# A hybrid decoder layer on one core: low halves and gated sums in turns, a key split and pooling products moved

## The reference, cut to what matters

```python
z = h @ lp['w_in']                       # one combined projection, h = x*(1+s1)+b1
att = forget_attention(q, k_all, v_all, ...)          # 8 heads x 64, prompt causal
conv_out = gb * dwconv3(gc * z_h)                     # 512 channels
pooled = trailing means over 2/4/8/16 tokens - token  # 4 groups of 128 channels
pool_out = einsum(pooled, lp['pool_w']) * lp['pool_scale']
gates = sigmoid(z[..., OFF_G:])                       # 3 gates of 1024 channels
merged = gates0*(att @ w_br_attn) + gates1*(conv_out @ w_br_conv) + gates2*(pool_out @ w_br_pool)
out = merged @ lp['w_o']
x = layer_norm(ALPHA * x + g1 * out)
x = layer_norm(ALPHA * x + g2 * SwiGLU(x*(1+s2)+b2))
```

## Time and profile before

| | us |
|---|---|
| median of 3 runs | 2202.35 (2200.02 to 2204.29) |
| profiled execution, its own time | 2206.09 |
| its span, first to last instruction | 2204.5 |
| PE busy (share of span) | 2047.4 (93%) |
| DVE, POOL, ACT busy | 797.4, 631.7, 389.2 |
| mean granted clock of PE | 0.966 |

### The profile page before, as it was taken

The page is one execution under the profiler, slowest core; times in us unless marked ns, Lnnn a source line. Parts: engine busy times, 40 slices in busy tenths (PEclk is TensorE's granted clock), DMA queues, the critical chain, the costliest instruction groups (busy, mean ns, idle before and its releaser), DMA issues.

```text
span 2204.5 us, 33007 instructions
## 1 busy us (share of the span) xinstructions
PE 2047.4 (93%) x13046; PEld 1941.9 (88%) x13046; DVE 797.4 (36%) x1423; ACT 389.2 (18%) x700; POOL 631.7 (29%) x482
## 2 busy tenths in 40 slices
PE   4989898778899999999999899999999999999996
PEld 3978887544599999999999798999999999999996
DVE  2445445543200042201702547333243323341326
ACT  1434444412110000000110124200000000000003
POOL 5031111042222232323332625323223232232323
PEclk9999998879999999999999899999999999999998
DMA  9232112167523112222111221011111111111112
GB/s 293 95 92 59 30 40 79 42 222 239 178 81 120 39 46 80 79 75 86 46 39 48 67 101 30 29 48 47 39 48 38 48 47 39 48 38 48 48 29 82
DMA packets 175721, 164.18 MB, mean 74 GB/s; under 512 B 15134, under 2 KB 139506, under 8 KB 175499
## 3 DMA queue, kind: packets, MB, share of 16 engines
q1 hardware_dynamic: 153307, 132.50, 19.7%
q0 software_dynamic: 6144, 17.01, 2.4%
q10 hardware_dynamic: 16184, 13.46, 2.0%
HBM read 149.03 MB, written 14.03 MB: 74 GB/s over the span
## 4 chain that ended last, share of the span: by engine, by line
PE 83%; DVE 6%; DMA 3%; SPq 3%; ACT 2%; issue 2%; POOL 1%; ACTq 0%; POOLq 0%; DVEq 0%
PE psA L1699 10%; PE psA L1705 10%; PE psA L1703 10%; PE psB L1705 10%; PE psB L1703 10%; PE psB L1699 10%; DMA kpage<-in_cache_k 2%; PE psB L1965 2%; PE psB L1808 2%; PE ps L1876 1%; PE psA L1862 1%; PE psB L1811 1%; PE psB L1812 1%; DVE prob L1241 1%; PE ps L1931 1%
## 5 line engine op out<-in xcount | busy, mean ns | idle before, releaser
L618 POOL CAST whi<-raw 128x1024 fp32r<-128x1024 f32 x131 | 136.0, 1038 | 1194.1 <-PE psA L1699 568.2
L619 POOL TENSOR_TENSOR wlo<-raw,whi 128x1024 fp32r<-128x1024 f32 x131 | 318.6, 2432 | 10.5
L1699 PE MATMUL psA<-hhi,whi 128*128 128x364 f32 x984 | 218.5, 330 | 4.2 <-DVE alo L1464 2.7
L1705 PE MATMUL psA<-hhi,wlo 128*128 128x364 f32 x984 | 218.8, 331 | 0.0
L1703 PE MATMUL psA<-hlo,whi 128*128 128x364 f32 x984 | 218.3, 330 | 0.0
L1705 PE MATMUL psB<-hhi,wlo 128*128 128x364 f32 x984 | 217.3, 329 | 0.0
L1703 PE MATMUL psB<-hlo,whi 128*128 128x364 f32 x984 | 217.3, 329 | 0.0
L1699 PE MATMUL psB<-hhi,whi 128*128 128x364 f32 x984 | 216.5, 328 | 0.0
L1699 PEld LDWEIGHTS psA<-hhi,whi 128*128 128x128 f32 x984 | 171.1, 189 | 5.0 <-issue 4.7
L1584 DVE TENSOR_TENSOR ft<-psB,sil 128x1092 f32<-128x1092 f32 x22 | 28.5, 1295 | 406.3 <-PE psB L1705 399.4
L1705 PEld LDWEIGHTS psA<-hhi,wlo 128*128 128x128 f32 x984 | 172.3, 189 | 0.0
(11 more groups left out here) (417 smaller groups left out, 3682.2 us busy)
## 6 DMA issues: line engine op xcount, KB each, us to landing
raw<-in_w_in SPq DMA_DIRECT2D x53, 512.0 KB, 3.9
raw<-in_w_gate_up SPq DMA_DIRECT2D x44, 512.0 KB, 3.8
kpage<-in_cache_k SPq DMA_DIRECT2D x64, 256.0 KB, 4.2
vpage<-in_cache_v POOLq DMA_DIRECT2D x64, 256.0 KB, 4.1
ada_late<-in_ada_w SPq DMA_DIRECT2D x8, 2048.0 KB, 8.0
raw<-in_w_down SPq DMA_DIRECT2D x22, 512.0 KB, 3.7
ada<-in_ada_w SPq DMA_DIRECT2D x4, 2048.0 KB, 17.5
x_keep<-xt SPq DMA_DIRECT2D x1, 4368.0 KB, 13.8
```

The source lines that it names most:

```text
L618: link(nc.gpsimd.tensor_copy(whi[slot][:, 0:n, :], raw[slot][:, 0:n, :]))
L619: nc.gpsimd.tensor_tensor(wlo[slot][:, 0:n, :], raw[slot][:, 0:n, :], whi[slot][:, 0:n, :].bitcast(F32), ALU.subtract).then_inc(s["w_split ...
L1699: m = mm(ps[:, c, 0:CH], whi[slot][:, b, :], hi[:, k, c * CH:(c + 1) * CH], start=first, stop=False)
L1705: m = mm(ps[:, c, 0:CH], wlo[slot][:, b, :], hi[:, k, c * CH:(c + 1) * CH], start=False, stop=last)
```

## The change

Three orders are changed; no computation is added or removed.

1. Output projection: the sums of tiles 4 and 5 leave `branch(2)` on DVE, and stand with those of tiles 6 and 7 among the low halves: two low halves, sum 4, two low halves, sum 5, low half 4, sum 6, low halves 5 and 6, sum 7 and its low half as before.
2. Attention: on DVE the second piece of `fill` at odd n comes after the two normalisations, not before.
3. Pooling: product 0 goes to `psB` ahead of the second gate unit, this unit to `psA`, then products 1, 2 and 3 to `psB`, `psA`, `psB` (`POOL_HALF`). ACT scales product 0 ahead of the second sigmoid. The branch's first gate unit waits for three low halves, not four.

```diff
--- before.py
+++ after.py
@@ -48,6 +48,7 @@
 NT = HALF // P
 POOL_WIN = (2, 4, 8, 16)
 POOL_ORDER = (3, 2, 1, 0)
+POOL_HALF = (1, 1, 0, 1)
 PST = 15
 LEAD = 16
 FF = 2816
@@ -1023,15 +1024,21 @@
                     last_rows(j - 1)
                 act.wait_ge(s["pf_done"], j + 1)
                 nc.scalar.copy(ahi[:, g, :], yp[:, :]).then_inc(s["phi_done"], 1)
+            def pool_scaled(j):
+
+                g = POOL_ORDER[j]
+                act.wait_ge(s["gemm_done"], 5 + j + 1)
+                nc.scalar.activation(c3(ahi[:, g, :]), cols(GP[POOL_HALF[j]]), ACT.Copy,
+                                     scale=vecs[:, V_PS + g:V_PS + g + 1]).then_inc(s["mhi_done"], 1)
+
             for k, x in enumerate("AB"):
                 act.wait_ge(s[f"g{x}"], 9)
-                nc.scalar.activation(c3(sgl[k][:, :]), cols(GP[k]), ACT.Sigmoid).then_inc(s[f"sg{x}"], 1)
+                nc.scalar.activation(c3(sgl[k][:, :]), cols(GP[0]), ACT.Sigmoid).then_inc(s[f"sg{x}"], 1)
                 if k == 0:
                     last_rows(NT - 1)
-            for j, g in enumerate(POOL_ORDER):
-                act.wait_ge(s["gemm_done"], 5 + j + 1)
-                nc.scalar.activation(c3(ahi[:, g, :]), cols(GP[j % 2]), ACT.Copy,
-                                     scale=vecs[:, V_PS + g:V_PS + g + 1]).then_inc(s["mhi_done"], 1)
+                    pool_scaled(0)
+            for j in range(1, NT):
+                pool_scaled(j)
             act.wait_ge(s["plo_done"], NT)
             gates(2)
 
@@ -1282,9 +1289,9 @@
                     ahead = (p, n + 1) if n + 1 < NTILE else (p + 1, 0)
                     for r in range(2 if ahead[0] < HP else 0):
                         scores_max(ahead[0], ahead[1] + r)
-                    next(fill, None)
                     for r in range(2 if ahead[0] < HP else 0):
                         normalise(ahead[0], ahead[1] + r)
+                    next(fill, None)
 
             dve.wait_ge(s["o_copied"], NTILE * HP)
             V.tensor_copy(alo[:, :, TU:T], zeros[:, :].rearrange("p (a b) -> p a b", a=NT)).then_inc(s["ol_done"], 1)
@@ -1461,21 +1468,32 @@
                 dve.wait_ge(s["plo_done"], j + 1)
             for j, g in enumerate(POOL_ORDER):
                 dve.wait_ge(s["mhi_done"], j + 1)
-                V.scalar_tensor_tensor(out=c3(alo[:, g, :]), in0=cols(GP[j % 2]), scalar=vecs[:, V_PS + g:V_PS + g + 1],
+                V.scalar_tensor_tensor(out=c3(alo[:, g, :]), in0=cols(GP[POOL_HALF[j]]), scalar=vecs[:, V_PS + g:V_PS + g + 1],
                                        in1=c3(ahi[:, g, :].bitcast(F32)), op0=ALU.mult, op1=ALU.subtract).then_inc(s["mlo_done"], 1)
-            branch(2, 3)
+            branch(2, 2)
 
             def merged_low(k, at, n):
 
                 dve.wait_ge(s["hhi_done"], KD + n)
                 V.tensor_tensor(hlo[:, k, at], merged[:, k, at], hhi[:, k, at].bitcast(F32), ALU.subtract).then_inc(s["hlo_done"], 1)
 
-            for k in range(KD - 2):
+            def gated_sum(x, turn, k, gate):
+
+                dve.wait_ge(s[f"b{x}"], turn)
+                to = part["AB".index(x)]
+                link(V.tensor_tensor(c3(to[:, :]), cols(GP["AB".index(x)]), c3(gate[:, :]), ALU.mult))
+                V.tensor_tensor(merged[:, k, :], merged[:, k, :], to[:, :], ALU.add).then_inc(s[f"m{x}"], 1)
+
+            for k in range(2):
                 merged_low(k, slice(0, T), k + 1)
-            dve.wait_ge(s["bA"], 12)
-            link(V.tensor_tensor(c3(part[0][:, :]), cols(GP[0]), c3(sgl[0][:, :]), ALU.mult))
-            V.tensor_tensor(merged[:, KD - 2, :], merged[:, KD - 2, :], part[0][:, :], ALU.add).then_inc(s["mA"], 1)
-            merged_low(KD - 2, slice(0, T), KD - 1)
+            gated_sum("A", 11, 4, sg[0])
+            for k in range(2, 4):
+                merged_low(k, slice(0, T), k + 1)
+            gated_sum("B", 11, 5, sg[1])
+            merged_low(4, slice(0, T), 5)
+            gated_sum("A", 12, KD - 2, sgl[0])
+            for k in (5, KD - 2):
+                merged_low(k, slice(0, T), k + 1)
             dve.wait_ge(s["bB"], 12)
             for n, (c0, c1) in enumerate(((0, 2), (2, 3))):
                 at = slice(c0 * CH, c1 * CH)
@@ -2045,19 +2063,23 @@
                 gemm(u0 % RING, GP[g % 2], all_k, done=s["gemm_done"])
                 if g:
                     last_rows(g - 1)
-            for k, x in enumerate("AB"):
-                u0 = U_POOL + NT + k
-                unit(u0)
-                gemm(u0 % RING, GP[k], all_k, done=s[f"g{x}"], free=((s["pcopied"], NT - 1 + k),))
-                if k == 0:
-                    last_rows(NT - 1)
-            u0 = U_POOL + NT + 2
-            unit(u0)
-            for j, g in enumerate(POOL_ORDER):
-                pe.wait_ge(s["mlo_done"] if j >= 2 else s["sgB" if j else "sgA"], j - 1 if j >= 2 else 9)
+            def pooled(j, sem_, n):
+
+                u0, g = U_POOL + NT + 2, POOL_ORDER[j]
+                pe.wait_ge(sem_, n)
                 pe.wait_ge(s["plo_done"], j + 1)
-                gemm(u0 % RING, GP[j % 2], [(g, g)], ahi, alo, done=s["gemm_done"], begin=j == 0)
-            branch(2, U_BRP, (s["mlo_done"], NT), (s["mlo_done"], NT), ((s["mlo_done"], NT),))
+                gemm(u0 % RING, GP[POOL_HALF[j]], [(g, g)], ahi, alo, done=s["gemm_done"], begin=j == 1)
+
+            unit(U_POOL + NT)
+            gemm((U_POOL + NT) % RING, GP[0], all_k, done=s["gA"], free=((s["pcopied"], NT - 1),))
+            last_rows(NT - 1)
+            unit(U_POOL + NT + 2)
+            pooled(0, s["pcopied"], NT)
+            gemm((U_POOL + NT + 1) % RING, GP[0], all_k, done=s["gB"], free=((s["sgA"], 9),))
+            pooled(1, s["mlo_done"], 1)
+            pooled(2, s["sgB"], 9)
+            pooled(3, s["mlo_done"], 2)
+            branch(2, U_BRP, (s["mlo_done"], NT - 1), (s["mlo_done"], NT), ((s["mlo_done"], NT),))
             unit(U_BRP + 9)
             for k, x in enumerate("AB"):
                 gemm((U_BRP + 9) % RING, GP[k], [(2 * t + k, t) for t in range(NT)], ahi, alo, done=s[f"b{x}"],
```

## The result

The changed kernel takes 2173.74 us (median of 4 runs, 2171.35 to 2174.6), the kernel before 2203.32 beside it (4 runs, 2200.02 to 2208.94): ratio 0.9862, 95% interval 0.9847 to 0.9876. A second set gave 2174.25 and 2203.8: 0.9874 (0.9855 to 0.9893). The forecast was 2178 and a gain of 24.4 us. The medians of both sets differ by 29.6 us; the second set's ratio stands for 27.8.

A forecast was written before the change was run, and what follows sets the result against it. TensorE holds 83% of the chain of waits, so only its idle or low-clock time can be won. 13 + 4.0 + 4.8 + 1.6 + 1.0 = 24.4 us off 2202.35 gives 2178, range 2171 to 2187.

The forecast's parts named there:

- Before the output projection: Ahead of the output projection: PE's 10.79 us wait goes, plus 2.3 us of low clock; 13 us, bounds 9 to 13.5.
- 1.2 us and the rest of POOL's instruction: DVE ahead of the output projection: each low half or add costs about 1.2 us plus what remains of POOL's running instruction.
- the rival of mere stretching: Ahead of the output projection: DVE instructions are stretched, 2.2 us each; PE loses 1 + 2 + 1, total 2182; chance 0.10.
- Pooling: Pooling stage: 3.0 us from reordered products and 1.0 from the clock; 4.0 us, bounds 1 and 4.6.
- The clock's part: Pooling stage, behind the branch's begin: 8 matmuls at clock 0.50 return to full clock, giving 1.0 us.
- its list of signs: Trace signs that would show the forecast right; for pooling, one 1.3 us wait for the third low half, branch at full clock.
- The rival, that the wait only moves to product 3: Pooling stage: product 3's wait grows to the sum of today's two; gain 1 instead of 4, total 2181; chance 0.10.
- Attention: Attention: 4.8 us from the keys' split, 1.6 from the query's last chunk, 1.0 in all from the clock.
- some 2: Attention, keys' split: of 3.66 us idle, 1.6 goes and some 2 us stays as a wait for the probabilities' low half.
- the split: Attention: moving the keys' split (2.1 us of DVE) behind two normalisations saves 1.6 us, three times: 4.8; upper bound 8.1.
- the query chunk: Attention, query's last chunk: the 1.08 us wait goes but its low half comes later; 0.55 three times, 1.6; bounds 0 and 3.2.
- rival 5: Output projection: the reload of x lands late among weight loads and stops PE, slower than before (2232 us); chance 0.04.

The follow-up runs named there:

- the old order: Three kernels without the attention swap (the kernel before, output projection's edit alone, pooling edit alone); head pairs 2 to 4 took 220.7 to 221.2 us.
- the changed order: Five executions with the attention swap (changed kernel twice, attention's edit alone, sums first, reload late); head pairs 2 to 4 took 213.5 to 214.8 us.

## Why the prediction was right, step by step

**Before the output projection: forecast 13, measured 13.2,** alone and together with the rest. With 17.85 us added (the distance of the last sigmoids), the changed trace gives the steps' ends as forecast: low halves 0 and 1 at 1231.8 (1231.9), 2 and 3 at 1236.8 (1236.9), tile 6's sum at 1248.3 (1248.2), low half 6 at 1250.8 (1250.6), the reload's issue at 1259.6 (1259.5). One step came 2.3 us earlier than counted: tile 5's sum, 1240.3 for 1242.67, since its add began before POOL's subtraction and made that one wait. The price "1.2 us and the rest of POOL's instruction" carried the forecast; the rival of mere stretching (a loss of 4) is out, since the two low halves with no POOL instruction beside them took 2.50 us together and the one behind a subtraction 3.50 alone. The kernel with all sums first shows what the turns are worth.

**Pooling: forecast 4.0, measured 4.54.** The idle time went from 1.23 + 2.74 to 1.16, so 2.81 less for the forecast 3.0, and the branch began 5.92 us behind the second gate unit's end for the forecast 5.85. (The wait left is for product 1's low half, the second one, as in the prediction's working; its list of signs calls it the third.) The clock's part was sized too small: 1.73 us came back for the 1.0 counted. The rival, that the wait only moves to product 3, is out.

**Attention: forecast 7.4 (4.8 + 1.6 + 1.0), measured 8.0** as the mean over the kernels in either order. The wait that was to stay under another name, "some 2" us for the low half, is 2.07, and the chunk's is 0.49 where 0.53 were left. In idle time the split gave 2.71 + 0.95 - 2.07 = 1.59 in two pairs and 1.07 in the first (the forecast counted 1.6 three times), the query chunk 0.59 a pair. So the waits of this mechanism give 6.0 for the forecast 6.4. But the 8.0 divides otherwise than forecast: averaged over the executions in either order PE's idle time in the attention fell by 5.2 us (41.0 to 35.8) and its busy time by 2.8 (266.4 to 263.6), for 6.4 and 1.0 in the forecast. That the sum came within 0.6 is partly luck. The clock gave 1.7 each in pairs 2 and 3 of the first two traces, where it held; pair 4, which I had not thought of, was 1.3 longer in four executions of the five (57.7 for 56.4 in the old order), and in the fifth it was the other way round.

**The sum: forecast 24.4, by stages 8.0 + 4.5 + 13.2 = 25.7, by the medians 29.6.** The 25.7 lies inside the second set's interval (23.6 to 32.0) and 1.6 below the first's (27.3 to 33.7). The rest is not attributed. Of the three edits alone, the attention's is where medians and stages differ most: 12.3 us by the medians (8.1 to 17.8 by the ratio), 8.0 by the stages. The stretch between attention and pooling holds the same instructions in all kernels and took 669.0 to 682.0 us in fourteen profiled executions, most of the spread in PE's busy time at clocks of 0.96 to 0.98 (649.0 against 639.4 us busy in the longest and one of the shortest, which differ by 12.7). Its mean is 674.5 in the three kernels in the old order and 672.3 in the other eleven; whether the edits move it, this many runs can't tell.

**The reload (rival 5)** had 4.9 us to spare for the forecast 5.4, and held.

## What to carry to other kernels

Where an engine makes several things for the same reader, price each one with its cover (here 1.2 us and the rest of the neighbour's instruction) and lay them in the order in which they are read; 13 us came from the order alone. If a stop can't be removed, shorten it: splitting a fill step, so that its ready part runs in idle time, brought the stop from 2.07 us to 1.08, and the clock held in nine of nine pairs. And compare stages over several executions before a clock term is named: two single traces said 11.1 us where eight together say 8.0.

## What the runs showed of the hardware that I had not expected

- After a stop of PE of 2.07 us the granted clock stayed at 1.00 in nine pairs of the changed order and fell in six (0.79 over the next 8 us in the first pairs, 0.57 over the next 4 in one of the others), with the same instructions in the same order. After 1.08 us it stayed in all nine, after 2.80 us it fell in two of three, after 3.5 us in all three. What tips it at 2 to 3 us stays open.
- A stretch that no edit touched can change with the clock: pair 4 took 54.10 us at 0.87 in one execution of the changed order and 57.4 to 58.1 at 0.79 to 0.82 in the four others. In those four, pairs 2 and 3 had run at 1.00, in the one at 0.98; but other kernels do not follow this, so the cause stays open.
- VectorE and GpSimd hold each other up in both directions: DVE's low half 3.50 us for 1.2, POOL's subtraction 3.49 for 2.40, by which of them had started first.
